# Latent attention: the queries' sums moved behind the first query products, the first values ahead of the first scores, weight units split up to two ahead, and two projection units with late slices

## What is computed

```python
h = x @ w_in
c_q, c_kv, k_r = jnp.split(h, [MLA_Q_LORA, MLA_Q_LORA + MLA_KV_LORA], axis=-1)   # 512, 256, 64
c_q = rms_norm(c_q, q_norm)
c_kv = rms_norm(c_kv, kv_norm)
q = (c_q @ w_uq).reshape(B, S, MLA_HEADS, MLA_NOPE + MLA_ROPE)                   # 16 heads, 128 + 64
q_nope = q[..., :MLA_NOPE]
q_rope = apply_rope(q[..., MLA_NOPE:], cos[:, :, None], sin[:, :, None])
k_rope = apply_rope(k_r, cos, sin)
k_nope = (c_kv @ w_uk).reshape(B, S, MLA_HEADS, MLA_NOPE)
v = (c_kv @ w_uv).reshape(B, S, MLA_HEADS, MLA_V)
for blk in range(S // Q_BLOCK):                                                  # 4 blocks of 128 queries
    s = (jnp.einsum('bqhd,bkhd->bhqk', q_nope[:, q0:q1], k_nope[:, :q1])
         + jnp.einsum('bqhr,bkr->bhqk', q_rope[:, q0:q1], k_rope[:, :q1])).astype(jnp.float32) * scale
    s = jnp.where(mask[:, None], s, NEG_INF_2)
    pr = jax.nn.softmax(s, axis=-1).astype(v.dtype)
    outs.append(jnp.einsum('bhqk,bkhd->bqhd', pr, v[:, :q1]))
return (o @ w_o).astype(x.dtype)
```

## Time and profile before

| | |
|---|---|
| Median of 3 runs | 2869.83 us (2864.10 to 2876.53) |
| The profiled execution | 2873.58 us, its span 2870.6 us |
| TensorE matmuls busy | 2759.5 us (96%) |
| VectorE busy | 1671.1 us (58%) |
| ScalarE busy | 1013.0 us (35%) |
| GpSimd busy | 340.7 us (12%) |
| Mean granted clock of TensorE | 0.97 of 2.4 GHz |
| DMA | 244.03 MB, 85 GB/s over the span |
| The chain that ended last | PE 85%, DVE 10%, ACT 3% |

### The profile page before, as it was taken

One profiled execution on the slowest core, in us unless ns is written; L12 is line 12 of the kernel. 1 busy time (PEld: TensorE's weight loads), 2 busy tenths in 40 slices (PEclk: granted clock), 3 DMA queues, 4 the chain that ended last, 5 costly groups with the idle time before them and its releaser, 6 DMA issues.

```text
span 2870.6 us, 35496 instructions
## 1 busy us (share of the span) xinstructions
PE 2759.5 (96%) x14739; PEld 2295.6 (80%) x14739; DVE 1671.1 (58%) x2541; ACT 1013.0 (35%) x1620; POOL 340.7 (12%) x351
## 2 busy tenths in 40 slices
PE   7999999999999999998999999999999979999998
PEld 6999999876688888875667688788878848878887
DVE  6755746466556534454655567647654356764765
ACT  3222233233334212233442344324343223542434
POOL 1144413110000000020000040000320004000031
PEclk9999999899899999997999999999999979999999
DMA  4233344420033333221121122332222202233222
GB/s 137 85 120 115 103 146 135 124 67 16 30 118 106 91 93 103 86 73 42 43 66 41 59 81 88 96 103 85 85 89 76 87 0 81 96 88 103 85 85 74
DMA packets 292727, 244.03 MB, mean 85 GB/s; under 512 B 19837, under 2 KB 285575, under 8 KB 292567
## 3 DMA queue, kind: packets, MB, share of 16 engines
q1 hardware_dynamic: 282503, 226.40, 25.3%
q0 software_dynamic: 5616, 13.22, 1.5%
q10 hardware_dynamic: 4448, 2.16, 0.3%
HBM read 230.70 MB, written 13.14 MB: 85 GB/s over the span
## 4 chain that ended last, share of the span: by engine, by line
PE 85%; DVE 10%; ACT 3%; issue 1%; DMA 1%; POOL 0%; ACTq 0%; SPq 0%; DVEq 0%; POOLq 0%
PE ps L562 24%; PE ps L563 24%; PE ps L564 24%; PE ps L1767 2%; DVE ul L550 2%; PE ps L2214 2%; PE ps L2213 2%; DVE rbuf L712 1%; PE ps L697 1%; PE ps L2289 1%; DVE tmp L2068 1%; ACT uh L535 1%; PE ps L1737 1%; PE ps L2261 1%; PE ps L2964 1%
## 5 line engine op out<-in xcount | busy, mean ns | idle before, releaser
L550 DVE TENSOR_TENSOR ul<-raw,uh 128x1024 fp32r<-128x1024 f32 (+3 forms) x416 | 528.9, 1293 | 346.1 <-ACT uh L535 345.6
L562 PE MATMUL ps<-OH,uh 128*128 128x512 f32 (+1 forms) x1704 | 643.3, 378 | 33.3 <-DVE ul L550 12.0
L563 PE MATMUL ps<-OL,uh 128*128 128x512 f32 (+1 forms) x1704 | 636.2, 373 | 0.0
L564 PE MATMUL ps<-OH,ul 128*128 128x512 f32 (+1 forms) x1704 | 635.8, 373 | 0.0
L535 ACT CAST uh<-raw 128x1024 fp32r<-128x1024 f32 (+3 forms) x416 | 412.3, 1025 | 166.2 <-PE ps L564 109.9
L562 PEld LDWEIGHTS ps<-OH,uh 128*128 128x128 f32 x1704 | 323.6, 190 | 99.3 <-DVE ul L550 15.3
L564 PEld LDWEIGHTS ps<-OH,ul 128*128 128x128 f32 x1704 | 323.9, 190 | 56.2
L563 PEld LDWEIGHTS ps<-OL,uh 128*128 128x128 f32 x1704 | 323.9, 190 | 55.9 <-issue 1.4
L562 PE MATMUL ps<-HH,uh 128*128 128x512 f32 (+2 forms) x946 | 321.8, 340 | 11.3 <-DVE HL L2652 11.3
L562 PE MATMUL ps<-XH,uh 128*128 128x264 f32 (+1 forms) x992 | 313.2, 316 | 11.0 <-DVE ul L550 6.8
L563 PE MATMUL ps<-HL,uh 128*128 128x512 f32 (+2 forms) x946 | 321.6, 340 | 0.0
(11 more groups left out here) (425 smaller groups left out, 3808.6 us busy)
## 6 DMA issues: line engine op xcount, KB each, us to landing
raw<-in_ffn_w SPq DMA_DIRECT2D x40, 1024.0 KB, 5.1
raw<-in_ffn_w_up SPq DMA_DIRECT2D x40, 1024.0 KB, 5.0
raw<-in_ffn_w SPq DMA_DIRECT2D x32, 704.0 KB, 4.5
raw<-in_ffn_w_down SPq DMA_DIRECT2D x32, 704.0 KB, 4.5
raw<-in_w_in SPq DMA_DIRECT2D x16, 1024.0 KB, 5.3
raw<-in_gla_w_in SPq DMA_DIRECT2D x12, 1024.0 KB, 5.1
raw<-in_mla_w_o SPq DMA_DIRECT2D x8, 1024.0 KB, 5.1
raw<-in_ple_w_gate SPq DMA_DIRECT2D x8, 1024.0 KB, 5.8
```

Of the source, the lines that this page charges most:

```text
L550: e.tensor_tensor(l, src, h.bitcast(F32), SUB).then_inc(*s_wlo.up(("unit", u)))
L562: e.matmul(o, wh, xh, start=first, stop=False)
L563: e.matmul(o, wh, xl, start=False, stop=False)
L564: return e.matmul(o, wl, xh, start=False, stop=last)
```

## The change

- The plan has the first value unit behind the first uk unit, ahead of the second uq unit.
- `query_norm_pe` runs behind `queries_pe(0)`; ACT's and DVE's parts of it move behind their shares of the queries. `cq_over`, which guards the tiles that QN, KN and QR overwrite, now waits for the last square in place of the sums.
- The values of pair 0 are computed at i = 0, behind the sums and ahead of the scores of head 0, and no longer at i = 2.
- `feed_hi` and `feed_lo` split two units ahead at the second cq unit, at every uq unit, at every uk unit but pair 1's, and in parts of the last projection.
- The first two units of the last projection go through `lin_late`: slices 0 to 5 of both, then slices 6 and 7 of each.

```diff
--- before.py
+++ after.py
@@ -211,8 +211,9 @@
         if p < 8:
             add("uq", kview(A["mla_w_uq_2"][0], 0, 4, p * 384, 384), 4, 384, [(0, 384, "heads")])
             add("uk", kview(A["mla_w_uk_2"][0], 0, 2, p * 256, 256), 2, 256, [(0, 256, 1)])
-        if p:
-            add("uv", kview(A["mla_w_uv_2"][0], 0, 2, p * 256 - 256, 256), 2, 256, [(0, 256, 1)])
+        if p != 1:
+            v = max(p - 1, 0)
+            add("uv", kview(A["mla_w_uv_2"][0], 0, 2, v * 256, 256), 2, 256, [(0, 256, 1)])
         if p == 5:
             mat("mo", A["mla_w_o_2"][0], 0, 8, 0, 1024)
     mat("mo", A["mla_w_o_2"][0], 1024, 8, 0, 1024)
@@ -2058,7 +2059,7 @@
 
             s_mm.wait_ge(e, ("cq", 3, 0))
             s_lo.wait_ge(e, ("xq", 3))
-            s_mm.wait_ge(e, "qss")
+            s_fn.wait_ge(e, ("xq", "sq", 3))
 
         def rope_dve(e, key, dst, what):
             s = tmps[3 + (0 if what == "kr" else 1 + key[1] % 3)][:, 0:512]
@@ -2107,7 +2108,7 @@
                     *s_fn.up(("xk", "sq", c, 0)))
             feed_hi(e, "cq")
             root(e, "xk", H2, 1.0 / 256, EPS5)
-            feed_hi(e, "cq")
+            feed_hi(e, "cq", 2)
             scaled("xk", XK, 2, 512, CK, "mla_kv_norm", 1)[0](e)
             for c in range(4):
                 if c > 1:
@@ -2132,7 +2133,7 @@
             feed_lo(e, "cq")
             rope_dve(e, ("kr", 0), KU, "kr")
             inverse(e, "xk", H2)
-            feed_lo(e, "cq")
+            feed_lo(e, "cq", 2)
             scaled("xk", XK, 2, 512, CK, "mla_kv_norm", 1)[1](e)
             kr_over(e)
             e.tensor_tensor(KR[:, :], KU, R0, MUL).then_inc(*s_dv.up("KR"))
@@ -2166,31 +2167,31 @@
             lin(e, "uk", XK, H2, ("kn", p, 1), cols=(128, 256), u=u)
 
         def queries_act(e, p):
-            feed_hi(e, "uq")
+            feed_hi(e, "uq", 2)
             if p:
                 s_mm.wait_ge(e, ("ms", 2 * p - 1))
             else:
-                query_norm_act(e)
                 cq_over(e)
             for hh in range(2):
                 s_mm.wait_ge(e, ("qn", p, hh, 0))
                 e.copy(QN[:, hh, :], P(("qn", p, hh, 0))).then_inc(*bk.free(s_cp, ("qn", p, hh, 0), ("qn", p, hh)))
-            feed_hi(e, "uk")
+            feed_hi(e, "uk", 1 if p == 1 else 2)
             for hh in range(2):
                 s_mm.wait_ge(e, ("kn", p, hh, 0))
                 e.copy(KN[:, hh, :], P(("kn", p, hh, 0))).then_inc(*bk.free(s_cp, ("kn", p, hh, 0), ("kn", p, hh)))
+            if p == 0:
+                query_norm_act(e)
 
         def queries_dve(e, p):
-            feed_lo(e, "uq")
+            feed_lo(e, "uq", 2)
             if p:
                 s_mm.wait_ge(e, ("ms", 2 * p - 1))
                 if p > 2:
                     s_dv.wait_ge(e, ("rope", "qr", p - 3, 0))
             else:
-                query_norm_dve(e)
                 cq_over(e)
             rope_dve(e, ("qr", p, 0), QR[:, :], "qr")
-            feed_lo(e, "uk")
+            feed_lo(e, "uk", 1 if p == 1 else 2)
 
         def latent_values_act(e, p):
             feed_hi(e, "uv")
@@ -2305,6 +2306,10 @@
 
         def latent_project_pe(e, half):
             for c in range(5 if half else 8):
+                if half and c < 2:
+                    if c == 0:
+                        lin_late(e, "mo", (OH, OL, "o1"), H2, range(8), (("mproj", 1, 0), ("mproj", 1, 1)), 2)
+                    continue
                 lin(e, "mo", (OH, OL, f"o{half}"), H2, ("mproj", half, c))
                 if half and c == 2:
                     layer_shift_pe(e, "x10")
@@ -2312,13 +2317,16 @@
         def latent_project_act(e, half):
             early = layer_early_act(e, "h1", "x10")
             for c in range(8):
-                feed_hi(e, "mo", 2 if half and c == 7 else 1)
+                feed_hi(e, "mo", 2 if half else 1)
                 if half:
                     early(c)
 
         def latent_project_dve(e, half):
+            if half:
+                feed_lo(e, "mo", 2)
             for c in range(5 if half else 8):
-                feed_lo(e, "mo")
+                if half == 0 or c:
+                    feed_lo(e, "mo", 2 if half and c == 2 else 1)
                 s_mm.wait_ge(e, ("mproj", half, c, 0))
                 if half:
                     s_dv.wait_ge(e, ("mh", 0, c) if c < 3 else ("x10", "c", c))
@@ -2346,13 +2354,15 @@
             latent_first_pe(e)
             bk.limit(4)
             for i in range(19):
+                if i % 2 == 0 and i < 16:
+                    queries_pe(e, i // 2)
                 if i == 0:
                     query_norm_pe(e)
-                if i % 2 == 0 and i < 16:
-                    queries_pe(e, i // 2)
                 if i >= 3:
                     latent_output_pe(e, i - 3)
-                if i % 2 == 0 and 2 <= i <= 16:
+                if i == 0:
+                    lin_tok(e, ("uv",), XK, [0, 128, 256, 384], 256, ("uv", 0))
+                if i % 2 == 0 and 4 <= i <= 16:
                     lin_tok(e, ("uv",), XK, [0, 128, 256, 384], 256, ("uv", i // 2 - 1))
                 if i == 10:
                     latent_project_pe(e, 0)
@@ -2373,7 +2383,9 @@
                     queries_act(e, i // 2)
                 if i >= 3:
                     latent_output_act(e, i - 3)
-                if i % 2 == 0 and 2 <= i <= 16:
+                if i == 0:
+                    latent_values_act(e, 0)
+                if i % 2 == 0 and 4 <= i <= 16:
                     latent_values_act(e, i // 2 - 1)
                 if i == 10:
                     latent_project_act(e, 0)
@@ -2393,7 +2405,10 @@
                     queries_dve(e, i // 2)
                 if i >= 3:
                     latent_output_dve(e, i - 3)
-                if i % 2 == 0 and 2 <= i <= 16:
+                if i == 0:
+                    feed_lo(e, "uv")
+                    query_norm_dve(e)
+                if i % 2 == 0 and 4 <= i <= 16:
                     feed_lo(e, "uv")
                 if i == 10:
                     latent_project_dve(e, 0)
```

## The result

| | before | changed |
|---|---|---|
| Median | 2867.64 us (2864.10 to 2876.53, 4 runs) | 2835.38 us (2829.16 to 2842.54, 4 runs) |
| Profiled execution | 2873.58 us | 2839.88 us |
| Ratio of times | | 0.9885, 95% interval 0.9857 to 0.9913 |

The change makes the kernel faster by 1.15%, 32 us.

What follows compares the result with a forecast made beforehand. TensorE was busy nearly all the span, so only its idle or low-clock time could be won. Gains of 18.2 (opening), 3.4 (splitting ahead) and 1.3 (end), together 22.9 off 2873.6, gave 2850.7 us; range 2843 to 2866.

Steps and rivals of the forecast that it cites:

- Queries of pair 0 with their keys: Opening: query and key products directly after the fourth cq unit, priced as 60 matmuls at full clock, 13.6 us.
- Queries 1: 13.6: Opening, behind scores 0 and 1: query and key products of pair 1, priced at 13.6 us.
- Low clock costs more than idle: Old opening: the low clock behind waits costs more than the idle; scores 0 and 1 took 9.1 and 10.9, not 5.77 us.
- Rival A: Opening: full clock holds through scores 0 to 3, giving the forecast time of 2851 us; chance 0.50.
- B: Clock falls in the new wait at i=2, slowing scores 2 and 3: 2864.6 us in full, 2858 if half; chance 0.35.
- Rival C: Opening: the clock's fall at the sums lasts into scores 0 and 1, returning 8.5 us: 2859 us; chance 0.07.
- Rival D: Splitting ahead makes ScalarE wait for loads ahead of the QN and KN copies: slower, 2901 us; chance 0.04.
- E: Slower: the falls at i=2 and at the sums come together, 22.4 us given back, 2873 us; chance 0.04.
- Units split further ahead: Iterations 4 to 14: value units' low half made before the rotation, so values start earlier; gain 3.4 us, bounds 0 and 5.9.
- The end: Last projection: the 1.12 us wait goes because that unit's low half is made earlier; gain 1.3 us.
- Late slices at nothing: Last projection's first two units: the first matmul waits for its bank, so the 1.49 us wait stays; gain 0.
- The four waits for OL: Four middle iterations: OL's correction frees the fourth value tile's bank later, 0.5 us of new wait each.

Runs made afterwards that it cites:

- the repeat: The changed kernel itself timed again with nothing altered, twelve runs: median 2838.16 us, ratio 0.9898 to the kernel before.
- experiment 4: Changed kernel with plain products for the first two mo units in place of the late slices; one execution, 2834.65 us.
- experiment 5: Changed kernel with the PSUM bank count starting at 4 behind the loop: 2827.88 us; with plain products for the first two mo units as well: 2839.48 us.
- experiment 2: Changed kernel with only the values of pair 0 back at i=2, sums still behind the key products; one execution, 2841.40 us.
- experiment 1: Changed kernel with sums ahead of the query products and values of pair 0 at i=2 again: 2838.88 us once, then twelve runs, median 2849.84 us, ratio 0.9940.

## Why the prediction was right and wrong

**The step that failed** is "Queries of pair 0 with their keys: 60 x 0.227 = 13.6". The price was right and the count was wrong. Three query products of four slices and two key products of two slices are 16 slices, and with three passes 48 matmuls: 10.9 us. The trace shows 48 in 11.1 us. The term stands twice in the sum, as "Queries 1: 13.6" again, so the new opening was made 2 x 2.7 = 5.4 us too long and the gain that much too small. The 12 too many in each are key products: where the prediction names the keys alone it has them right, with 2.7 us for 12. And the trace of the kernel before had the count. Its queries and keys of pairs 0 and 1:

```profile
1307.90:1320.90 13.00, 13.00 (x49) 10.38 (x49) 2.70 (x6) 3.49 (x6) 0.00 (x0) 0.84 0.00 0
1343.60:1356.00 12.40, 12.40 (x49) 9.85 (x48) 4.69 (x7) 3.60 (x7) 0.00 (x0) 0.89 0.07 22
```

Their lengths come near 13.6, but only because part of each ran at the lower clock: 13.0 x 0.84 is 10.9 and 12.4 x 0.89 is 11.0, which is 48 matmuls. So a rebuild of the old opening from the same terms, with its low clock added, would have come out 5.4 us over what the trace shows. I rebuilt only the new one.

The count explains 5.4 of the 15.6 us between 2851.0 and 2835.4. Another 5.9 is **the starting point**: the sum was taken off the profiled execution, "I don't subtract the 3.75", and the kernel before has a median of 2867.64, 5.9 under that execution. The last 4 us are the difference between a gain of 28.3 and the 32.3 of the first comparison; no stretch of the latent attention shows them. The right count alone would have moved the range to 2838 to 2861, still above 2835.4; the 2838.2 of the repeat would lie barely inside.

The other terms, against the changed profile:

| Step | predicted | measured |
|---|---|---|
| Fourth cq unit with its wait | 5.4 + 0.6 | 5.94 (0.34 of wait) |
| Queries and keys of pair 0 | 13.6 | 11.2 |
| Sums | 3.6 | 3.5 |
| First values, low clock included | 3.0 + 1.2 | 4.2 |
| Scores 0 and 1 | 11.5 | 11.9 |
| Queries and keys of pair 1 | 13.6 | 11.0 |
| From the keys to scores 2 (idle in it) | 2.7 (1.6) | 2.6 (1.2) |
| Opening, gain | 18.2 | 22.9 |
| Units split further ahead | 3.4 | 3.7 |
| The end | 1.3 | 1.4 |

With 48 in place of 60 the sum is 28.3 us, where the stretches give 28.0. It puts the profiled execution at 2845.3. The measured 2839.9 lies 5.4 us lower: 5.7 from outside the three stretches, less the 0.3. The repeat with more runs did not show them again (28.0 us between the medians).

- *Low clock costs more than idle.* Right for the profiled executions: in the opening TensorE is busy 14.5 us less with the same matmuls and idle 8.4 less. It is not so in every execution: with sums and values back, a net 2.9 us more idle, one opening was 6.1 us longer and another 15.6.
- *Rival A against B.* A happened in the profile of the changed kernel; B happened in two of the seven profiles that have the wait ahead of scores 2 (experiments 4 and 5), near the 0.35 given to it. Five of those seven have identical instructions up to it, and the two falls are among the five. So A or B is indeed a matter of each execution, at 6.5 us.
- *Rival C.* It came about only without the values (experiment 2). The half chance given to a fall at the sums was too small: it came in seven of nine profiles with the sums in one piece ahead of the values, and was over with them or just behind.
- *Rival D.* Didn't happen. Among ScalarE's waits from 1285 to 1640 us none is for a load, and the middle is shorter. Nor did E: no profile has B and C together.
- *Late slices at nothing.* Right, with its reason: the first unit waited for its bank. Freeing the bank gave 1.7 us.
- *The four waits for OL.* Predicted 0.5 each, measured 0.42.
- *The range.* It covered what the clock might do and the 3.7 us of the median, and nothing for a wrong count.

## What to carry to other kernels

Price a rearrangement by rebuilding the old stretch and the new one from the same terms; when the old one doesn't come out at its measured length, a count or a price is wrong. Multiply a measured stretch by its granted clock before comparing it with a full-clock price, and take the forecast off the median, not off one execution. Look behind each idle for the clock that the next products run at, and put products that recover quickly, not those that stay slow, behind a place where it falls. When a wait stays although the data have been there for long, look who holds the PSUM bank that comes next in turn: a shifted start of the count may be all that is needed.

## What the runs showed of the hardware that was not expected

- **Busy is not enough.** One-column matmuls (0.11 us each) kept TensorE busy for 3.5 us, and the clock fell behind them in eight of ten profiles that have them in one piece behind the query and key products. In pieces of a quarter, a quarter and a half of that between query products it didn't fall, but that is one profile against two of ten that have no fall with the one piece. That the columns are the cause was not tried.
- **Products differ in how they recover.** At the lower level, scores of 128 to 512 columns stayed there for 22.0 us (experiment 2); value products took at most 4.5 us for what takes 3.0 at full clock, and scores 0 behind them ran at 0.96 or more; the query products behind those slow scores lost 2.6 us and were out; and after one slow head (10.0 us) full clock was back behind the 4.63 us of an output (experiment 4). What in the products makes the difference was not tried.
- **The same instructions meet different clocks.** Behind a wait of 2.5 us, scores 0 and 1 took 11.7 us in one execution and 19.7 in another of the same code (experiment 1). The Trainium skill (TensorE: Matmul & The Clock Gate, Part 1) has the gate's looks free-running; the falls at i = 2 in two of five profiles with the same instructions agree with that.
